# Two transformer blocks on one core: how the first input, the tables and the first matmuls are started

## The chip, the cores and the metric

The kernel runs on one core of a Trainium2 chip. The metric is the device time of one execution in microseconds. TensorE (PE) multiplies matrices, VectorE (DVE), ScalarE (ACT) and GpSimd (POOL) work element by element, and SyncE (SP) issues transfers. Transfers issued by SyncE and by ScalarE go into two queues (q1 and q10 in the profile), which the core's 16 DMA engines serve.

## The reference, cut to what matters

Two transformer blocks work one after the other on 1024 tokens of width 1024, in float32. Only the very beginning of the first block concerns this change:

```
n = rms_norm(x, attn_norm_w)      # x * rsqrt(mean(x * x) + eps) * w
proj = n @ w_in                   # keys, values, queries, retention heads, gates
aq, ak, av, rq, rk, rv, rg = split(proj)
aq, ak = rope(rms_norm(aq, q_norm_w)), rope(rms_norm(ak, k_norm_w))
```

After it come windowed attention, retention, an output projection, a feed-forward layer, and a second block with dilated attention, a gating unit, cross attention and a feed-forward layer.

## The kernel before, in words

**Layout.** The activations lie transposed: H is 128 partitions x 8 tiles (`kt`) x 1024 tokens. Tokens are worked on in two halves of 512 (`half(0)`, `half(1)`). `x_piece(t, q)` is a quarter of a tensor of that shape: q = 0 and 1 are tiles 0 to 3 and 4 to 7 of the first half of the tokens, q = 2 and 3 the same of the second. One piece is 1.05 MB, and each partition's rows in it are 2 KB long. ROPE (rotation tables) is 128 x 2 x 1024 floats, BD a 128 x 128 table, IDENT another, ONES 8 columns, VEC 117 columns. A unit of weights is 128 x 1024 floats, 0.52 MB.

**Precision.** Every float32 product is made of three fast matmuls. Each operand is split into a high part, rounded to the type of the fast matmul, and a low part, what is left. For a tile: WH x XH, WL x XH, WH x XL. GpSimd splits the weights (`split_unit`, L821 makes WH, L823 WL, a half unit at a time). ScalarE makes XH (`x_highs`, L1793 inside `high`), scaled by the norm's weight, and VectorE XL (`x_lows`, L2561 inside `low`), which needs XH. The division by the root of the mean square comes later, since it is one factor per token.

**First pass.** `first_units` (L1038, L1039, L1041) multiplies units 0 (keys) and 1 (values). For each half of the tokens it goes through the tiles with the two units side by side, the second unit three tiles behind the first: 48 matmuls per half. Ahead of the second half's first tile stand the column sums of squares of the first half (`norm_sums`, L1052), and ahead of its seventh tile the spreading of the reciprocal root over the partitions (`norm_spread`, L1071). TensorE's instructions run strictly in the order written.

**Orders on the other engines.** ScalarE: the issues of VEC, IDENT, ONES, the four pieces of H, BD and ROPE (L1821 to L1827), then high parts 0 and 1, squares 0 and 1 (L1839), high parts 2 and 3, square 2, the root, square 3. Its first real instruction loads an activation table (ACT_TABLE_LOAD). VectorE: four small edits of VEC (L2595 to L2598), low parts 0 and 1, the sums of squares 0 and 1 (L2608 to L2614), low parts 2 and 3, sum 2, a reciprocal, sum 3, then the evictions of the first pass (L2643). GpSimd: splits of units 0 and 1, and then one unit after another, each when TensorE has finished with that buffer. SyncE: units 0 and 1 (L734), then the next ones (L737), each after the split of the unit two before.

**Semaphores.** `vec_in` counts VEC, IDENT and ONES, and TensorE, ScalarE, VectorE and GpSimd all begin with a wait on it. `x_part[q]` tells that piece q of H is in. `x_in` is used much later for a reload of H (L2009, waited on at L3081). `dve_step` counts VectorE's own `link` steps. PS bank MB is the one that the column sums use later.

Of the kernel before, what the change touches and what calls it, by code (L numbers as in the profile page):

```python
# [23 lines left out]
ACT = mybir.ActivationFunctionType  # L24
# [3 lines left out]
P = 128  # L28
# [183 lines left out]
V_EPS = 114  # L212
# [4 lines left out]
C_ID, C_BD, C_ONE, C_MASK = 0, 128, 256, 384  # L217
# [86 lines left out]
def program(nc, xT, memT, ws, vec, cst, rope, bias, wsp, bsg, outT):  # L304
# [3 lines left out]
    def sem(name):  # L308
        return ctx.enter_context(nc.semaphore(name))

    with ctx:

        def sb(stack, name, shape, dt=F32):
            return stack.enter_context(nc.sbuf_tensor(name, shape, dt))
# [15 lines left out]
        SQ = sb(ctx, "SQ", [P, 2, HALF])  # L330
        XX = sb(ctx, "XX", [P, 2048])
        STAT = sb(ctx, "STAT", [P, 96])

        with ExitStack() as st:
# [7 lines left out]
            ROPE = sb(st, "ROPE", [P, 2, S])  # L342
            PT1 = sb(st, "PT1", [P, 3, 2 * P])
            BD = sb(st, "BD", [P, P])
# [14 lines left out]
        with ExitStack() as st:  # L359
            H = sb(st, "H", [P, KT, S])  # L360
# [47 lines left out]
        PS = ctx.enter_context(nc.psum_tensor("PS", [P, 8, HALF], F32))  # L408
        SB, OB, MB = 4, 6, 7
# [3 lines left out]
        def v(col, n=1):  # L413
            return VEC[:, col:col + n]

        def half(h):
            return slice(h * HALF, (h + 1) * HALF)
# [7 lines left out]
        vec_in, x_in, rope_in, mask_in, cst2_in, xr_in = map(sem, ("vec_in", "x_in", "rope_in", "mask_in", "cst2_in", "xr_in"))  # L425
        x_in2, bias_in0, bias_in1, sgu_in, mem_in = map(sem, ("x_in2", "bias_in0", "bias_in1", "sgu_in", "mem_in"))
        h_out, y_out = map(sem, ("h_out", "y_out"))
        x_part = [sem(f"x_part{q}") for q in range(4)]
# [12 lines left out]
        act_step, dve_step = map(sem, ("act_step", "dve_step"))  # L441
        vec_ready, blocks_in = map(sem, ("vec_ready", "blocks_in"))
# [90 lines left out]
        def x_piece(t, q):  # L533
            return t[:, 4 * (q % 2):4 * (q % 2) + 4, half(q // 2)]
# [51 lines left out]
        for g in range(3):  # L586
            q = 2 * (12 * g + 14)
# [144 lines left out]
        def _(sp):  # L732
            for j in range(2):
                sp.dma_start(WRAW[:, j], ws[WS_AT[j]]).then_inc(raw_in[j], 16)  # L734
            for u in range(2, U_RK):
                sp.wait_ge(unit_split, 2 * u - 2)
                sp.dma_start(WRAW[:, u % 2], ws[WS_AT[u]]).then_inc(raw_in[u % 2], 16)  # L737
# [249 lines left out]
        def _(pe):  # L987
# [101 lines left out]
                    unit_half(u, h, first_half_norm(k, 4, 6) if h else None)  # L1089


            pe.wait_ge(vec_in, 48)

            def scores1(s):
# [364 lines left out]
            def scores2(s):  # L1459
                g, b, j = place(s)  # L1460
                _, K, _ = QKV[g % 2]
                Q = QKV[g % 2][0]
                if g:
# [167 lines left out]
            for n in range(1, 4):  # L1631
                for h in range(2):
# [5 lines left out]
                    for b in range(2):  # L1638
                        for kt in range(KT):
                            last = pe.matmul(PS[:, MB, b:b + 1], XX[:, kt * MEM + b * P:kt * MEM + (b + 1) * P], ONES[:, 0:1],  # L1640
                                             start=(kt == 0), stop=(kt == KT - 1))
                    last.then_inc(mem_sum, 1)
                if n == 2:
                    pe.wait_ge(mem_inv, 1)
                    for b in range(2):
                        last = pe.matmul(PS[:, MB, blk(b)], STAT[:, 42 + b:43 + b].to_broadcast((P, P)), IDENT,
                                         start=True, stop=True)
# [125 lines left out]
        def _(act):  # L1773
# [18 lines left out]
            def high(dst, src, scale=1.0):  # L1792
                act.activation(dst, src, ACT.Copy, scale=scale).then_inc(x_high, 1)  # L1793
                nx.n += 1
# [26 lines left out]
            act.dma_start(VEC[:], vec).then_inc(vec_in, 16)  # L1821
            act.dma_start(IDENT, cst[:, C_ID:C_ID + P]).then_inc(vec_in, 16)
            act.dma_start(ONES, cst[:, C_ONE:C_ONE + NKEEP - P]).then_inc(vec_in, 16)
            for q in range(4):
                act.dma_start(x_piece(H, q), x_piece(xT, q)).then_inc(x_part[q], 16)
            act.dma_start(BD[:], cst[:, C_BD:C_BD + P]).then_inc(blocks_in, 16)
            act.dma_start(ROPE[:], rope).then_inc(rope_in, 16)  # L1827

            def x_highs(q):

                act.wait_ge(x_part[q], 16)
                for i in range(4):
                    kt, h = 4 * (q % 2) + i, half(q // 2)
                    high(XH[:, kt, h], H[:, kt, h], v(V_N1 + kt))

# [7 lines left out]
                act.activation(RST[h], PS[:, OB + h], ACT.Copy).then_inc(rst_made, 1)  # L1843

            act.wait_ge(vec_in, 48)
            x_highs(0)
            x_highs(1)
            x_square(0)
            x_square(1)
            x_highs(2)  # L1850
            x_highs(3)
            x_square(2)
# [472 lines left out]
            def copy_mb(k, n):  # L2325
                item = MB_USES.get(k, (None, None))[n]
                if item is None or item[0] == "mix":
                    return
                act.wait_ge(m_full, nm.n + 1)
                nm.n += 1  # L2330
                src = PS[:, MB].rearrange("p (a b) -> p a b", a=4)
                if item[0] == "v":
                    _, g, t, c = item
                    dst = QKV[g % 2][2][:, 4 * c:4 * c + 4, blk(t)]
                else:
                    _, t, c = item
                    dst = VS[:, 4 * c:4 * c + 4, blk(t)]
                act.activation(dst, src, ACT.Copy).then_inc(m_free, 1)
# [194 lines left out]
        def _(dve):  # L2533
# [5 lines left out]
            def link(ins):  # L2539

                ins.then_inc(dve_step, 1)
                nst.n += 1
                dve.wait_ge(dve_step, nst.at())
# [44 lines left out]
                        XH[:, m % 8, half(m // 8)])  # L2588


            dve.wait_ge(vec_in, 48)
            lf = VEC[:, V_LF:V_LF + 8]
            lfb = VEC[:, V_LFB:V_LFB + 16]
# [484 lines left out]
                    else:  # L3078
                        last_outputs()

            dve.wait_ge(x_in, 16)  # L3081
            dve.wait_ge(x_in2, 16)
            residual(U_WO1, 1)
            ffn(0, 1, V_F1, last_result1)
# [363 lines left out]
```

## Time and profile before

| | us |
|---|---|
| median of 3 runs | 2755.48 |
| lowest and highest | 2753.03, 2758.49 |
| the profiled execution, span | 2756.5 |
| TensorE busy in the span | 2702.0 |

The times above are whole executions, and the profile is one execution of its own: its span runs from its first instruction to its last. A row of the timeline gives the start in us from the span's start, the length, the engine, the line, the operation, the operands and how many are merged. A "q" behind an engine's name is its sequencer issuing transfers. In brackets stands how long the engine was idle before, and what ended it.

### The profile page before, as it was taken

The numbers are of one execution on the slowest core, as the hardware profiler recorded it, in microseconds if no ns is written. First come the engines' busy times: TensorE is split into PE (matmuls) and PEld (weight loads), VectorE is DVE, ScalarE is ACT, GpSimd is POOL, SyncE is SP. The second block draws the span as 40 slices with busy tenths as digits, with TensorE's granted clock in tenths as the row PEclk, the third lists the DMA queues.
The fourth block names the chain that finished last, engine by engine and source line by source line (L and its number), as shares of the span: only waits on it lengthen the run. The fifth ranks groups of instructions, "written<-read, shape, count | busy, mean of one in ns | idle before, by whom it ended". The sixth has DMA issues, their size and how long they took to land.

```text
span 2756.5 us, 37485 instructions
## 1 busy us (share of the span) xinstructions
PE 2702.0 (98%) x13788; PEld 2191.8 (80%) x13788; DVE 1719.8 (62%) x2578; ACT 1059.7 (38%) x2084; POOL 1518.5 (55%) x1148
## 2 busy tenths in 40 slices
PE   7999999999999999999999999999999999999998
PEld 6777788878888888777777788888788788888886
DVE  6776755687777777723355741143368777767777
ACT  5644422343444444423343511021254444444444
POOL 3232243477887878532222244455614788787884
PEclk9999999999999999999999999999999999999999
DMA  3001102111111211130101011131101212121112
GB/s 136 31 31 37 38 17 92 54 54 58 58 62 58 69 54 58 51 117 31 39 32 40 32 46 54 53 122 62 69 24 46 65 53 63 58 70 54 58 54 80
DMA packets 102774, 157.18 MB, mean 57 GB/s; under 512 B 6992, under 2 KB 60752, under 8 KB 101456
## 3 DMA queue, kind: packets, MB, share of 16 engines
q1 hardware_dynamic: 97472, 133.19, 14.5%
q10 hardware_dynamic: 5136, 21.76, 2.1%
q8 instruction: 106, 1.74, 0.3%
q14 instruction: 60, 0.49, 0.1%
HBM read 146.54 MB, written 8.39 MB: 56 GB/s over the span
## 4 chain that ended last, share of the span: by engine, by line
PE 91%; DVE 3%; POOL 2%; issue 1%; ACT 1%; DMA 1%; ACTq 0%; SPq 0%; DVEq 0%; POOLq 0%
PE PS L1346 13%; PE PS L1347 13%; PE PS L1348 13%; PE PS L1000 12%; PE PS L1002 11%; PE PS L1001 11%; PE PS L1120 1%; PE PS L1038 1%; PE PS L1041 1%; PE PS L1039 1%; PE PS L1109 1%; PE PS L1488 1%; PE PS L1380 1%; PE PS L1135 1%; PE PS L1374 1%
## 5 line engine op out<-in xcount | busy, mean ns | idle before, releaser
L821 POOL TENSOR_TENSOR WH<-WRAW,CST 128x512 fp32r<-128x512 f32 x204 | 226.5, 1110 | 838.9 <-PE PS L1002 725.7
L1000 PE MATMUL PS<-XH,WH 128*128 128x512 f32 x1248 | 513.4, 411 | 2.9 <-POOL WL L823 2.0
L1002 PE MATMUL PS<-XH,WL 128*128 128x512 f32 x1248 | 490.0, 393 | 0.0
L1001 PE MATMUL PS<-XL,WH 128*128 128x512 f32 x1248 | 488.8, 392 | 0.0
L3035 DVE TENSOR_TENSOR H<-H,PS 128x512 f32<-128x512 f32 x560 | 367.3, 683 | 41.9 <-PE PS L1348 41.7
L856 POOL TENSOR_TENSOR WL<-WRAW,WH 128x512 fp32r<-128x512 f32 x174 | 251.4, 1446 | 118.2 <-ACT WH L2058 88.8
L1000 PEld LDWEIGHTS PS<-XH,WH 128*128 128x128 f32 x1248 | 235.3, 189 | 82.8 <-issue 36.8
L823 POOL TENSOR_TENSOR WL<-WRAW,WH 128x512 fp32r<-128x512 f32 x204 | 271.3, 1330 | 16.0
L1002 PEld LDWEIGHTS PS<-XH,WL 128*128 128x128 f32 x1248 | 235.0, 188 | 51.4
L1001 PEld LDWEIGHTS PS<-XL,WH 128*128 128x128 f32 x1248 | 235.9, 189 | 41.9 <-issue 0.5
L856 POOL TENSOR_TENSOR WL<-XX,WH 128x512 fp32r<-128x512 f32 x148 | 202.0, 1367 | 92.9 <-ACT WH L2058 92.5
L1346 PE MATMUL PS<-XH,WH 128*128 128x512 f32 x640 | 249.5, 390 | 1.5 <-POOL WL L856 1.4
L1348 PE MATMUL PS<-XH,WL 128*128 128x512 f32 x640 | 249.2, 389 | 0.0
L1347 PE MATMUL PS<-XL,WH 128*128 128x512 f32 x640 | 249.2, 389 | 0.0
L1347 PE MATMUL PS<-PL,WH 128*128 128x512 f32 x624 | 243.2, 390 | 0.0
L1346 PE MATMUL PS<-PH,WH 128*128 128x512 f32 x576 | 224.7, 390 | 0.0
L1348 PE MATMUL PS<-PH,WL 128*128 128x512 f32 x576 | 224.3, 389 | 0.0
L1346 PE MATMUL PS<-TR,WH 128*128 128x512 f32 x480 | 187.9, 392 | 11.0 <-POOL WL L856 3.1
L1348 PE MATMUL PS<-TR,WL 128*128 128x512 f32 x480 | 187.4, 390 | 0.0
L1347 PE MATMUL PS<-TR,WH 128*128 128x512 f32 x480 | 187.4, 390 | 0.0
L2088 ACT ACTIVATE PH<-PV 128x512 fp32r<-128x512 f32 x140 | 88.2, 630 | 143.4 <-PE PS L1348 91.8
L1346 PEld LDWEIGHTS PS<-XH,WH 128*128 128x128 f32 x640 | 120.2, 188 | 27.5 <-issue 2.7
(371 smaller groups left out, 5416.0 us busy)
## 6 DMA issues: line engine op xcount, KB each, us to landing
WRAW<-ws SPq DMA_DIRECT2D x104, 512.0 KB, 3.5
WRAW<-ws SPq DMA_DIRECT2D x120, 256.0 KB, 2.6
XX<-ws SPq DMA_DIRECT2D x108, 256.0 KB, 2.7
RAWX<-ws SPq DMA_DIRECT2D x56, 256.0 KB, 2.6
H<-xT ACTq DMA_DIRECT2D x4, 1024.0 KB, 11.0
H<-xT ACTq DMA_DIRECT2D x2, 2048.0 KB, 11.1
h_spill<-H ACTq DMA_DIRECT2D x1, 4096.0 KB, 12.9
H<-h_spill ACTq DMA_DIRECT2D x4, 1024.0 KB, 8.5
```

The source lines that it names most:

```text
L821: pool.tensor_tensor(WH[:, j, c], WRAW[:, j, c], ONES[:, 0:1].to_broadcast((P, 512)), ALU.mult).then_inc(hi_split, 1)
L823: pool.tensor_tensor(WL[:, j, c], WRAW[:, j, c], WH[:, j, c].bitcast(F32), ALU.subtract).then_inc(unit_split, 1)
L856: pool.tensor_tensor(WLS[:, at], weight(s), WHS[:, at].bitcast(F32), ALU.subtract).then_inc(w_low, 1)
L1000: pe.matmul(out, WH[:, j, w], rh(kt), start=(n == 0), stop=False)
L1001: pe.matmul(out, WH[:, j, w], rl(kt), start=False, stop=False)
L1002: last = pe.matmul(out, WL[:, j, w], rh(kt), start=False, stop=(n == len(kts) - 1))
L1038: pe.matmul(PS[:, bank], WH[:, j, w], XH[:, kt, half(h)], start=(kt == 0), stop=False)
L1346: pe.matmul(PS[:, bank], WHS[:, at, w], xh, start=start and not on, stop=False, skip_group_check=on)
L1347: pe.matmul(PS[:, bank], WHS[:, at, w], xl, start=False, stop=False, skip_group_check=on)
L1348: return pe.matmul(PS[:, bank], WLS[:, at, w], xh, start=False, stop=stop, skip_group_check=on)
L2088: act.activation(PH[:, n % 2], value(name), ACT.Copy).then_inc(hid_high, 1)
L3035: dve.tensor_tensor(x, x, PS[:, 4 + t], ALU.add).then_inc(h_added, 1)
```

## The change

Five things are done together. The first piece of H comes in two transfers of two tiles each, with the semaphore `x_in` for the first (ScalarE waits for it, and for `x_part[0]` ahead of the third tile); the late wait on `x_in` goes up to 32. Pieces 2 and 3 of H, ROPE and BD are issued by SyncE right behind the first two units of weights, not by ScalarE. ScalarE runs one small copy as soon as the constants are in, before it waits for H. VectorE clears SQ[:, 0] first of all. And TensorE multiplies this cleared tile with itself five times, in plain float32 with 512 columns, into bank MB, before it waits for the constants.

```diff
--- before.py
+++ after.py
@@ -732,6 +732,10 @@
         def _(sp):
             for j in range(2):
                 sp.dma_start(WRAW[:, j], ws[WS_AT[j]]).then_inc(raw_in[j], 16)
+            for q in (2, 3):
+                sp.dma_start(x_piece(H, q), x_piece(xT, q)).then_inc(x_part[q], 16)
+            sp.dma_start(ROPE[:], rope).then_inc(rope_in, 16)
+            sp.dma_start(BD[:], cst[:, C_BD:C_BD + P]).then_inc(blocks_in, 16)
             for u in range(2, U_RK):
                 sp.wait_ge(unit_split, 2 * u - 2)
                 sp.dma_start(WRAW[:, u % 2], ws[WS_AT[u]]).then_inc(raw_in[u % 2], 16)
@@ -1089,6 +1093,9 @@
                     unit_half(u, h, first_half_norm(k, 4, 6) if h else None)
 
 
+            pe.wait_ge(dve_step, 1)
+            for n in range(5):
+                pe.matmul(PS[:, MB], SQ[:, 0, 0:P], SQ[:, 0], start=True, stop=True)
             pe.wait_ge(vec_in, 48)
 
             def scores1(s):
@@ -1821,15 +1828,16 @@
             act.dma_start(VEC[:], vec).then_inc(vec_in, 16)
             act.dma_start(IDENT, cst[:, C_ID:C_ID + P]).then_inc(vec_in, 16)
             act.dma_start(ONES, cst[:, C_ONE:C_ONE + NKEEP - P]).then_inc(vec_in, 16)
-            for q in range(4):
-                act.dma_start(x_piece(H, q), x_piece(xT, q)).then_inc(x_part[q], 16)
-            act.dma_start(BD[:], cst[:, C_BD:C_BD + P]).then_inc(blocks_in, 16)
-            act.dma_start(ROPE[:], rope).then_inc(rope_in, 16)
+            act.dma_start(H[:, 0:2, half(0)], xT[:, 0:2, half(0)]).then_inc(x_in, 16)
+            act.dma_start(H[:, 2:4, half(0)], xT[:, 2:4, half(0)]).then_inc(x_part[0], 16)
+            act.dma_start(x_piece(H, 1), x_piece(xT, 1)).then_inc(x_part[1], 16)
 
             def x_highs(q):
 
-                act.wait_ge(x_part[q], 16)
+                act.wait_ge(x_in if q == 0 else x_part[q], 16)
                 for i in range(4):
+                    if (q, i) == (0, 2):
+                        act.wait_ge(x_part[0], 16)
                     kt, h = 4 * (q % 2) + i, half(q // 2)
                     high(XH[:, kt, h], H[:, kt, h], v(V_N1 + kt))
 
@@ -1843,6 +1851,7 @@
                 act.activation(RST[h], PS[:, OB + h], ACT.Copy).then_inc(rst_made, 1)
 
             act.wait_ge(vec_in, 48)
+            act.activation(STAT[:, 57:58], v(V_EPS), ACT.Copy)
             x_highs(0)
             x_highs(1)
             x_square(0)
@@ -2588,6 +2597,7 @@
                         XH[:, m % 8, half(m // 8)])
 
 
+            link(dve.memset(SQ[:, 0], 0.0))
             dve.wait_ge(vec_in, 48)
             lf = VEC[:, V_LF:V_LF + 8]
             lfb = VEC[:, V_LFB:V_LFB + 16]
@@ -3078,7 +3088,7 @@
                     else:
                         last_outputs()
 
-            dve.wait_ge(x_in, 16)
+            dve.wait_ge(x_in, 32)
             dve.wait_ge(x_in2, 16)
             residual(U_WO1, 1)
             ffn(0, 1, V_F1, last_result1)
```

## Rows read from the trace of the kernel before

**Rows 1.** The page: span, and its section 4, the chain's shares by engine.
```profile
span 2756.5 us, 37485 instructions
...
PE 91%; DVE 3%; POOL 2%; issue 1%; ACT 1%; DMA 1%; ACTq 0%; SPq 0%; DVEq 0%; POOLq 0%
```

**Rows 2.** Chain of waits in order of time, first 27 us: start us, us, what.
```profile
2.16 8.06 DMA H<-xT
...
10.29 1.28 ACT L1793
...
12.34 5.74 DVE XL L2561 x4
...
18.13 0.49 PE PS L1041
```

**Rows 3.** Waits of PE, 18 to 47 us: us in total, times, longest us.
```profile
PE PS L1041 <- DVE XL L2561: 0.7, 1, 0.7
```

**Rows 4.** Windows: length, busy us (instructions) per engine, PEclk, DMA share, GB/s.
```profile
6.50:11.00 4.50, 0.00 (x0) 0.00 (x0) 1.27 (x4) 0.71 (x1) 3.86 (x4) 1.00 1.02 374
...
16.00:20.70 4.70, 3.97 (x16) 2.63 (x15) 4.70 (x7) 4.70 (x4) 1.52 (x1) 1.00 1.04 407
```

**Rows 5.** DMA queues (packets, MB, share) for 0 to 6, 3.5 to 5, 0 to 8.5 us.
```profile
q1 hardware_dynamic: 287, 1.05, 46.4%
q10 hardware_dynamic: 469, 0.25, 16.6%
...
q1 hardware_dynamic: 145, 0.53, 87.9%
q10 hardware_dynamic: 124, 0.05, 13.2%
...
q10 hardware_dynamic: 938, 1.15, 42.2%
```

**Rows 6.** Timeline of ACT, its queue and SyncE's queue, up to 60 us.
```profile
5.78 3.48 ACTq L1826 DMA_DIRECT2D BD<-cst  x1
...
11.59 5.01 ACT L1793 ACTIVATE XH<-H,VEC 128x512 fp32r<-128x512 f32 x8
11.72 36.37 SPq L737 DMA_DIRECT2D WRAW<-ws  x4
...
20.11 5.00 ACT L1793 ACTIVATE XH<-H,VEC 128x512 fp32r<-128x512 f32 x8
```

**Rows 7.** Timeline of DVE, 12 to 36 us.
```profile
12.34 8.38 DVE L2561 SCALAR_TENSOR_TENSOR XL<-H,VEC,XH 128x512 fp32r<-128x512 f32 x8 [4.14 <-ACT XH L1793]
...
24.48 0.69 DVE L2614 TENSOR_TENSOR ACC<-ACC,ROOM 128x512 f32<-128x512 f32 x1
25.09 5.38 DVE L2561 SCALAR_TENSOR_TENSOR XL<-H,VEC,XH 128x512 fp32r<-128x512 f32 x8
...
35.61 0.69 DVE L2643 TENSOR_TENSOR ACC<-PS,RG 128x512 f32<-128x512 f32 x1 [0.62 <-ACT RG L1843]
```

**Rows 8.** Timeline of POOL, its first and its last split of units 0 and 1.
```profile
6.98 1.04 POOL L821 TENSOR_TENSOR WH<-WRAW,CST 128x512 fp32r<-128x512 f32 x1 [6.53 <-DMA CST<-cst]
...
15.90 1.62 POOL L823 TENSOR_TENSOR WL<-WRAW,WH 128x512 fp32r<-128x512 f32 x1
```

**Rows 9.** Timeline of PE: column sums, spreading, end of the last early wait.
```profile
26.67 0.95 PE L1052 MATMUL PS<-CST,ACC 128*128 128x1 f32 x8
...
33.73 1.05 PE L1071 MATMUL PS<-CST,STAT 128*128 128x128 f32 x8
...
59.38 1.02 PE L1155 MATMUL PS<-BD,RQ 128*128 128x2 f32 x8 [1.70 <-ACT V L1910]
```

**Rows 10.** Windows as in rows 4: PE's first eight matmuls, and after 59.38.
```profile
12.45:16.40 3.95, 3.91 (x8) 2.13 (x8) 3.95 (x4) 3.95 (x7) 3.79 (x4) 1.00 1.05 396
61.00:64.00 3.00, 3.00 (x9) 2.35 (x8) 2.82 (x5) 1.95 (x4) 0.21 (x1) 0.50 0.47 162
```

**Rows 11.** Chain of waits as in rows 2: a plain float32 product, 512 columns.
```profile
44.84 0.86 PE PS L1152 x2
```

## Prediction, made before the change was built or run

> **What bounds the kernel now.** I read the page first, the chain of work that ended last second, and then one timeline per engine for the first 60 us. The page gives a 2756.5 us span and TensorE 91% of the chain [rows 1]. So the body is a serial queue of matmuls, and an edit to the first microseconds pays what it moves the start of that unbroken queue, and no more. The chain's opening shows where the queue starts [rows 2]: ScalarE's queue issues the first piece of H, its landing takes until 10.22, ScalarE loads its table (1.28 us), makes the first high part (VectorE can start at 12.34), VectorE makes four low parts (until 18.08), and from 18.13 TensorE has one matmul after another. Between 18 and 47 us TensorE waited for an engine once, 0.7 us, and that is the wait that ends at 18.13 [rows 3]. So the start that counts is 18.13, not the 12.45 of the first matmul. Twelve of the first pass's 48 matmuls are done by then; the other 36, 0.23 us apart, end at 26.6, when the column sums begin (26.67) [rows 9]. After about 47 us TensorE waits for VectorE and ScalarE (the last wait ends 59.38) [rows 9], and those waits hang on results that TensorE gave just before.
>
> **What the transfers do.** This decides the case. From 6.5 to 11 and from 16 to 20.7 us the DMA engines move 374 and 407 GB/s at a busy share of 1.02 and 1.04: they are full [rows 4]. By 6.0 us the sync queue (q1) has moved its 1.05 MB, both weight units, while ScalarE's queue (q10) has moved 0.25 MB, of which the small tables (253 columns of 128 rows) are 0.13 [rows 5]. After that q10 has the engines alone. Its 1.18 MB (tables and first piece) are through at about 8.6 (1.15 MB at 8.5) [rows 5], but the piece counts as landed at 10.22 [rows 2]: a tail of 1.65 us, since all 16 engines must finish. The second piece, another 1.05 MB at 0.39 MB per us (between the two of [rows 4]), is through at 11.3 and lands near 12.8. ScalarE asks for it at 14.1, after four high parts of 0.63 us (eight in 5.01) [rows 6], so nobody waits for it.
>
> **The change, part by part.**
>
> First piece in two transfers. Its first half is 0.52 MB. At 6.0 us 0.12 MB of it are in and 0.40 MB are left.
>
> Later tokens (2.1 MB), the rotation table (1.05 MB) and the block table on the sync queue. The sync queue held no transfer of its own from 6.0 to the issue at 11.72 [rows 5, 6]; now it has the third piece right behind the weights. How do two full queues share the engines? From 3.5 to 5.0 us they moved 145 and 124 packets [rows 5]: nearly one to one. The pieces have equal packets (2 KB rows) on both queues, so each queue gets half the bytes, some 0.19 MB per us. Hence: first half through at 6.0 + 0.40 / 0.187 = 8.15, landed with the same tail at 9.8; second half 2.7 us on, landed 12.5; **second piece, another 1.05 / 0.197 = 5.3 us on, landed at 17.7 instead of 12.8.** The bounds are 12.8 (the sync queue starts late or gets nothing) and 19.4 (the tail twice as long); I take the even share, which is what the nearest row shows. The issue of five more transfers on SyncE costs nothing: its next one waits until 11.72 anyway [rows 6], and the unit it fetches is split by POOL only when TensorE has ended the unit in that buffer, after both passes (past 36 us). ScalarE loses the block table's issue (3.48 us) and the rotation table's behind it, which ended ahead of 10.2 and were covered by the landing [rows 6].
>
> The Trainium skill ("DMA: Bandwidth & Descriptors", section "Issuing engines are not separate DMA queues") says that DMAs started by different engines run on the same 16 DMA engines and interleave, and that issuing on several saves only the issuing time. The rows agree as to the interleaving, and it speaks against the move: no bandwidth is added, and the urgent second piece now shares with tokens that ScalarE reads only at 20.1.
>
> Table load early. The constants are in at 6.5 (POOL's first wait) [rows 8], so the 1.28 us load runs from 6.9 to 8.2 while the transfer is in flight. It leaves the path entirely: the first high part ends at 9.8 + 0.73 = 10.5 instead of 12.32, the 0.73 being the way from the table's end at 11.57 to there [rows 2].
>
> Spare matmuls. A call with f32 operands and 512 columns is two instructions here, and two took 0.86 us of the chain [rows 11]. Five are 4.3 us at full rate. The first eight matmuls of the kernel before took 3.95 us [rows 10], 0.43 us apart and more: half the 0.23 us rate or less, though the granted clock reads 1.00 there; at half rate the five take 8.6 us. They start behind a memset at about 1.1 us and end between 5.4 and 9.7: ahead of 10.5. They cost nothing, but gain little too: TensorE was waiting for VectorE at 18.13, with the eight slow ones long behind it [rows 2, 9]. The memset is under 1 us on an idle VectorE.
>
> **The sum.** Low parts: the first four took 1.44 us each on the chain beside POOL's splits, and 0.66 after those end at 17.5 [rows 2, 7, 8]. From 10.5 four are ready at 16.3, not 18.08. But then the second piece is missing. High part four is done at 17.7 + 0.75 = 18.45, and TensorE (15 of 48 matmuls done) goes on with 33 x 0.23 = 7.6 us plus 0.3 us of waiting for the first low part: 26.3. ScalarE: four highs until 20.25, squares (1.8 us apart) until 22.15 and 23.95, where both were over by 20.2, since the third piece's high parts begin at 20.11 [rows 6]. VectorE's column sums of the first half of the tokens can end only 2.6 us after 23.95, at 26.6, where they ended at 25.17 [rows 7]; TensorE needs them at 26.67 in its order, so it loses nothing there. Then eight low parts (5.3 us) to 31.9, the third sum to 33.75, the reciprocal to 33.9: TensorE wants it at 33.73 [rows 9] and loses 0.2 us. The fourth sum ends at 36.6, the first eviction starts 1.0 us later than its 35.61, and that is slack for TensorE, whose first product from it comes at 44.84 [rows 7, 11]. So the 1.8 us gained ahead of 12 us are given back while waiting for the second piece: net **+0.2 us**. Span 2756.5 becomes 2756.7. The profiled span lies 1.0 us above the median of the runs, 2755.48, and inside their 2753.03 to 2758.49, so the forecast is 2755.48 + 0.2 = 2755.7.
>
> **Rivals.** (a) The second piece comes in time. If the sync queue's new transfers hardly get in, as bound 12.8, ScalarE never stops; four low parts are done at 16.3 minus the half microsecond that the warm matmuls save, 15.8, and TensorE's 36 matmuls end at 24.1 to 24.4: 2.3 us sooner, about 2753.2. For it: the count of 145 to 124 comes from small packets beside large ones, not from equals. Against it: the sync queue's weights, issued at the same time, were moving at full tilt from the start, and nothing in the trace holds its next transfers back. (b) Slower. TensorE stands thinly used for the 8 us before 18.4. After its wait up to 59.38 [rows 9] the granted clock was 0.50 from 61 to 64 us [rows 10]. If the clock falls likewise before 18.4, some eight matmuls at 0.43 instead of 0.23 put 1.7 us on top of 26.3, so the first pass ends at 28.0, and TensorE is 1.3 us behind; with the second piece 1 us later still it is 2.5 us: 2757 to 2758. It decides as soon as the fall costs more than the 0.35 us between 26.3 and the column sums' 26.65. The Trainium skill ("TensorE: Matmul & The Clock Gate", section "HAM oscillation — how this bites in real kernels") says waits on DMA between bursts let the clock fall again; no row here shows it for gaps as short as these. (c) The change does not do what it says: the spare matmuls end after 10.5, or the early load is followed by a second one ahead of the high parts. It costs at most the 1.28 us gained and hides behind the second piece: 2755.7 again, or 2754.5 beside (a).
>
> **How the numbers follow.** Forecast 0.50, (a) 0.27, (b) 0.15, (c) 0.08. All lie within 3 us of the start. The bound of 0.2%, about what a measurement can tell from no change, is 5.5 us, so what crosses it is the scatter of runs (2.5 us below and 3.0 above the median) on top of (a) or (b): faster 0.07, same 0.88, slower 0.05. The range takes (a) less 1.7 and (b) plus 1.7: 2751.5 to 2759.5.
>
> **What would show it.** Right: the H pieces' longest landing on ScalarE's queue near 15 us after issue; ScalarE idle about 3 us ahead of its third and again its fifth high part, with DMA named as what ended the wait; TensorE idle until 18.4; column sums at about 26.6; the chain naming the H transfer twice. Wrong: second piece landed before 14 us, TensorE unbroken from 16 us, column sums by 24.5 (rival a); the granted clock or the spacing at half rate beyond 18 us (rival b). The whole would be wrong by more than these sizes only if something outside the first 60 us moved, which no part of the change touches.

## The result, and the profile after

The changed kernel is slower, by 0.2%. Its 16 executions have a median of 2762.14 us (2755.91 to 2766.81) against 2755.85 us (2752.97 to 2760.86) for 16 of the kernel before; the ratio is 1.002, with a 95% interval of 1.0013 to 1.0026. Run again (e5 below) it came to 2761.02 against 2755.38, ratio 1.0019 (1.001 to 1.0028). The forecast was 2755.7 us in a range of 2751.5 to 2759.5. All medians below leave out four executions, one each in e1, e9, e10 and e11, that took 3007 to 12302 us.

The profiled execution is one of the quicker ones: 2757.94 us, with a span of 2756.1. That execution lasted 1.8 us longer than its span, and the profiled execution of the kernel before, with its span of 2756.5, was the one of 2758.49 us, 2.0 us longer. The two spans can't be compared by themselves; the first 60 us can.

Chain of waits of the changed kernel, first 60 us (start us, us, what), beside [rows 2]:

```profile
2.16 1.03 ACTq L1831
3.22 0.64 ACTq L1832
3.89 16.26 DMA H<-xT
20.17 0.73 ACT XH L1800
21.04 0.66 PE PS L1042
21.70 0.43 PE PS L1043
...
24.68 0.23 PE PS L1045
...
30.39 0.79 PE PS L1056 x8
```

The chain no longer runs through the first piece of H. It runs through the second: issued at 3.89, landed at 20.15. TensorE's unbroken queue starts at 21.04, not 18.13, and its first matmuls are 0.43 us apart. The column sums come 3.6 us later than in [rows 9].

Timeline of ScalarE in the changed kernel, beside [rows 6]:

```profile
4.41 1.28 ACT L1854 ACT_TABLE_LOAD   x1 [4.41 <-issue]
7.90 0.20 ACT L1854 ACTIVATE STAT<-VEC 128x1 f32<-128x1 f32 x1 [2.21 <-DMA CST<-cst]
10.60 1.34 ACT L1800 ACTIVATE XH<-H,VEC 128x512 fp32r<-128x512 f32 x2 [2.50 <-DMA H<-xT]
13.41 1.34 ACT L1800 ACTIVATE XH<-H,VEC 128x512 fp32r<-128x512 f32 x2 [1.47 <-DMA H<-xT]
20.17 2.56 ACT L1800 ACTIVATE XH<-H,VEC 128x512 fp32r<-128x512 f32 x4 [5.42 <-DMA H<-xT]
```

The table load is off the path: it ran from 4.41, before the constants were in. The first high part starts 1 us earlier than 11.59. But ScalarE, which made eight high parts in one go before, now stands idle three times for a landing, the last time for 5.42 us.

TensorE in the changed kernel (the spare matmuls, the restart behind the second piece, and the column sums):

```profile
1.46 7.54 PE L1098 MATMUL PS<-SQ 128*128 128x512 f32 x10 [1.46 <-DVE SQ L2600]
...
21.04 0.66 PE L1042 MATMUL PS<-XH,WH 128*128 128x512 f32 x1 [2.85 <-ACT XH L1800]
...
24.48 0.44 PE L1045 MATMUL PS<-XL,WH 128*128 128x512 f32 x1
...
30.22 0.95 PE L1056 MATMUL PS<-CST,ACC 128*128 128x1 f32 x8
```

Windows of the changed kernel (columns as in rows 4):

```profile
21.00:24.40 3.40, 3.37 (x8) 2.59 (x9) 2.66 (x4) 3.40 (x4) 0.00 (x0) 0.52 0.29 116
```

The granted clock is 0.52 of full speed for the 3.4 us behind the restart, that is at its lower level, 1.2 GHz, after TensorE had stood from 18.2 to 21.04 and been busy for 2.0 of the 3 us ahead of that.

The queues of the changed kernel (packets, MB, share of the 16 engines), beside [rows 5]: in order 0 to 6 us, 6.5 to 11 us, 16 to 18 us.

```profile
q1 hardware_dynamic: 356, 1.19, 52.4%
q10 hardware_dynamic: 317, 0.13, 8.6%
...
q1 hardware_dynamic: 488, 0.97, 57.3%
q10 hardware_dynamic: 452, 0.80, 48.0%
...
q1 hardware_dynamic: 81, 0.66, 80.2%
q10 hardware_dynamic: 80, 0.16, 21.7%
```

These rows bear on the working of the landing. By 6.0 us ScalarE's queue has moved 0.13 MB, not 0.25: its small tables themselves went slower, since the sync queue never ran dry. They were in at 7.9 us, where they had been in at 6.9. From 6.5 to 11 us the bytes are shared nearly evenly, as forecast. From 16 to 18 us the packets are still shared one to one, 81 to 80, but not the bytes: 0.66 MB against 0.16. The mean packet on q1 is then 8 KB. That is the rotation table, whose rows are 8 KB each, against the 2 KB rows of the second piece of H.

### The profile page after: what moved, and what is told of

Its sections match the earlier page's. It is cut to its first block, busy times and chain, and to the rows that moved or that the text cites. A ratio compares the mean times of both kernels' runs of the same rounds, so it can differ in the third digit from the quotient of the medians.

```text
span 2756.1 us, 37508 instructions
## 1 busy us (share of the span) xinstructions
PE 2706.1 (98%) x13798; PEld 2190.4 (79%) x13798; DVE 1719.6 (62%) x2579; ACT 1060.1 (38%) x2085; POOL 1520.8 (55%) x1148
## 4 chain that ended last, share of the span: by engine, by line
PE 91%; DVE 3%; POOL 2%; issue 1%; ACT 1%; DMA 1%; ACTq 0%; SPq 0%; DVEq 0%; POOLq 0%
PE PS L1353 13%; PE PS L1354 13%; PE PS L1355 13%; PE PS L1004 12%; PE PS L1006 11%; PE PS L1005 11%; PE PS L1127 1%; PE PS L1042 1%; PE PS L1045 1%; PE PS L1043 1%; PE PS L1116 1%; PE PS L1495 1%; PE PS L1387 1%; PE PS L1142 1%; PE PS L1381 1%
## 6 DMA issues: line engine op xcount, KB each, us to landing
h_spill<-H ACTq DMA_DIRECT2D x1, 4096.0 KB, 12.5
```

## The experiments

Each kernel ran beside the kernel before, in four groups (e1 to e4; e5 to e8; e9 and e10; e11 and e12), so that differences of about 1 us between groups mean little. "Sums" is the start of the first column sums in the one execution that was profiled (26.67 before); "piece 1" is when the second piece of H was in, read from ScalarE's next high part.

| kernel | piece 1, us | sums, us | median against before, us | ratio (95% interval) |
|---|---|---|---|---|
| changed, first time | 20.15 | 30.22 | +6.3 | 1.002 (1.0013 to 1.0026) |
| e5, changed again | 20.73 | 29.75 | +5.6 | 1.0019 (1.001 to 1.0028) |
| e1, all but the move | in time | 27.68 | +1.1 | 1.0007 (0.9998 to 1.0017) |
| e2, the move alone | 20.26 | 29.89 | +4.3 | 1.0016 (1.0007 to 1.0025) |
| e3, spare matmuls alone | in time | 26.74 | +1.0 | 1.0003 (0.9994 to 1.0012) |
| e4, SyncE held for piece 1 | 12.15 | 25.39 | -2.2 | 0.9993 (0.9984 to 1.0002) |
| e6, changed, no spares | 21.06 | 32.44 | +5.9 | 1.0015 (1.0006 to 1.0024) |
| e7, e4 without spares | 12.14 | 24.33 | -2.8 | 0.9989 (0.998 to 0.9998) |
| e9, four more spares | 20.85 | 30.45 | +4.8 | 1.002 (1.0011 to 1.003) |
| e11, two more spares | 20.77 | 29.79 | +5.0 | 1.0014 (1.0005 to 1.0024) |
| e8, only tables held | 17.32 | 26.41 | +1.7 | 1.0007 (0.9998 to 1.0016) |
| e10, table in 2 KB rows | 19.36 | 28.38 | +2.1 | 1.0007 (0.9998 to 1.0017) |

For e5 the sums had been expected between 30.2 and 32.2 us, with half rate behind the restart. They came at 29.75 and TensorE was at full rate there, so that failed; the median, expected 4 to 7 us above before, held.

### Taking the change apart

The first question was whether the move of transfers or the spare matmuls cost the time. e1 takes the move out:

```diff
-            for q in (2, 3):
-                sp.dma_start(x_piece(H, q), x_piece(xT, q)).then_inc(x_part[q], 16)
-            sp.dma_start(ROPE[:], rope).then_inc(rope_in, 16)
-            sp.dma_start(BD[:], cst[:, C_BD:C_BD + P]).then_inc(blocks_in, 16)
...
             act.dma_start(x_piece(H, 1), x_piece(xT, 1)).then_inc(x_part[1], 16)
+            for q in (2, 3):
+                act.dma_start(x_piece(H, q), x_piece(xT, q)).then_inc(x_part[q], 16)
+            act.dma_start(BD[:], cst[:, C_BD:C_BD + P]).then_inc(blocks_in, 16)
+            act.dma_start(ROPE[:], rope).then_inc(rope_in, 16)
```

> All of the change but the move: pieces 2 and 3 of H, BD and ROPE stay on ScalarE's queue behind piece 1; the split first piece, the early table load, the memset and the five spare matmuls stay in. Theory 1 (the second piece of H lands late because the sync queue's transfers take half of the DMA engines): the second piece lands near 12.8 us instead of 20.2, the first column sums come at 24.4 to 24.8 us (before 26.67, changed kernel 30.39), and the time is 2 us below the kernel before. Theory 2 (the spare matmuls or the clock behind them cost the time): column sums stay near 30 us and the time stays some 4 to 6 us above the kernel before.

e2 is the kernel before with the move alone:

```diff
+            for q in (2, 3):
+                sp.dma_start(x_piece(H, q), x_piece(xT, q)).then_inc(x_part[q], 16)
+            sp.dma_start(ROPE[:], rope).then_inc(rope_in, 16)
+            sp.dma_start(BD[:], cst[:, C_BD:C_BD + P]).then_inc(blocks_in, 16)
...
-            for q in range(4):
+            for q in range(2):
                 act.dma_start(x_piece(H, q), x_piece(xT, q)).then_inc(x_part[q], 16)
-            act.dma_start(BD[:], cst[:, C_BD:C_BD + P]).then_inc(blocks_in, 16)
-            act.dma_start(ROPE[:], rope).then_inc(rope_in, 16)
```

> The kernel before with the move alone: pieces 2 and 3, ROPE and BD on the sync queue behind the first two units of weights; no split, no early table load, no spare matmuls. Theory 1: the first piece lands near 13.5 us instead of 10.2 and the second near 20; column sums at 30 us or later, time 3.5 to 6 us above the kernel before. Theory 2: column sums within 1 us of 26.67, time unchanged.

e3 is the kernel before with the memset and the spare matmuls alone:

```diff
+            pe.wait_ge(dve_step, 1)
+            for n in range(5):
+                pe.matmul(PS[:, MB], SQ[:, 0, 0:P], SQ[:, 0], start=True, stop=True)
             pe.wait_ge(vec_in, 48)
...
+            link(dve.memset(SQ[:, 0], 0.0))
             dve.wait_ge(vec_in, 48)
```

> The kernel before with the memset and the five spare matmuls alone. Theory 1: nothing is moved by more than 1 us; column sums between 26.0 and 26.7 us, time within 1 us of the kernel before. Theory 2: the time rises by 2 us or more, and the trace shows TensorE at half rate in a place where it runs at full rate in the kernel before.

The move costs 4.3 us by itself, with an interval clear of no change, and shows the late piece without any other part. Chain of waits and then ScalarE's timeline in e2:

```profile
2.16 11.08 DMA H<-xT
```

```profile
14.60 2.56 ACT L1797 ACTIVATE XH<-H,VEC 128x512 fp32r<-128x512 f32 x4
20.28 2.56 ACT L1797 ACTIVATE XH<-H,VEC 128x512 fp32r<-128x512 f32 x4 [3.12 <-DMA H<-xT]
```

The first piece lands at 13.24 and the second at 20.26; 13.5 and 20 were expected. The sums, expected at 30 or later, came at 29.89. The spare matmuls alone moved the column sums by 0.1 us, and their time can't be told from no change. So theory 1 stands and theory 2 falls as an account of the loss. But e1 missed its numbers: it should have been 2 us quicker than the kernel before and is not, and its sums came at 27.68, not at 24.4 to 24.8. ScalarE's timeline in e1 tells why:

```profile
5.45 1.60 ACTq L1832 DMA_DIRECT2D BD<-cst  x1
7.09 2.55 ACTq L1833 DMA_DIRECT2D ROPE<-rope  x1
9.67 1.28 ACT L1854 ACT_TABLE_LOAD   x1 [9.67 <-issue]
...
11.07 5.00 ACT L1796 ACTIVATE XH<-H,VEC 128x512 fp32r<-128x512 f32 x8
```

The issues of BD and ROPE held ScalarE until 9.64. In the kernel before the landing of the first piece covered them. With half a piece that lands sooner (8.2 us) they are the next thing late: the table load came at 9.67 all the same, and the first high part starts only 0.5 us earlier than before. And TensorE fell to half rate after the spare matmuls. Windows of e1 and of e3:

```profile
13.70:20.40 6.70, 6.03 (x14) 3.71 (x13) 6.70 (x8) 6.70 (x8) 3.50 (x3) 0.50 1.04 402
```

```profile
12.00:18.00 6.00, 5.92 (x12) 2.99 (x12) 6.00 (x5) 6.00 (x9) 5.15 (x4) 0.50 1.05 396
```

The spare matmuls are done at 8.7 and 7.7 us; TensorE is then idle for 3.2 and 4.2 us, and the clock is at its lower level when the real work comes, or soon after, for 6.8 us. In e1 that outlasts VectorE's slow low parts, and the column sums come 1 us later than before; that the half rate is the reason is read from the trace and wasn't tested by itself.

### Keeping the move, and letting the second piece go first

e4 adds one wait to the changed kernel, e7 takes the memset and the spare matmuls out of e4 as well:

```diff
+            sp.wait_ge(x_part[1], 16)
             for q in (2, 3):
                 sp.dma_start(x_piece(H, q), x_piece(xT, q)).then_inc(x_part[q], 16)
```

> The changed kernel with one wait more: SyncE issues pieces 2 and 3, ROPE and BD only when piece 1 has landed. Theory 1: piece 1 lands near 12.8 us, piece 2 near 18, column sums at 24.4 to 24.8 us, time about 2 us below the kernel before, as in the run with the pieces on ScalarE's queue. Theory 2: as the changed kernel, 4 to 6 us above the kernel before.

> The changed kernel with SyncE held until piece 1 has landed, and without the memset and spare matmuls. Theory 1a: column sums at 25.4 us or earlier (with the spare matmuls 25.39), the time 2 to 3 us below the kernel before. Theory 1b: column sums at 26 us or later.

e6 is the changed kernel without the memset and the spare matmuls, with its transfers as they are; e7 has this edit too.

```diff
-            pe.wait_ge(dve_step, 1)
-            for n in range(5):
-                pe.matmul(PS[:, MB], SQ[:, 0, 0:P], SQ[:, 0], start=True, stop=True)
...
-            link(dve.memset(SQ[:, 0], 0.0))
```

> The changed kernel without the memset and the five spare matmuls. Theory 1a (the spare matmuls only start the clock early, and it falls again before it is needed): column sums within 0.7 us of the changed kernel's 30.39, the time the same as the changed kernel's or up to 2 us less, because TensorE's first 15 matmuls then run at half rate while it waits anyway, and it is at full rate at 21. Theory 1b (they do help): column sums and time 1.5 us or more later than with them.

ScalarE's timeline in e7:

```profile
8.24 2.65 ACT L1798 ACTIVATE XH<-H,VEC 128x512 fp32r<-128x512 f32 x4 [1.37 <-DMA H<-xT]
12.16 2.57 ACT L1798 ACTIVATE XH<-H,VEC 128x512 fp32r<-128x512 f32 x4 [1.27 <-DMA H<-xT]
```

With SyncE's later transfers held, the small tables are in at 6.7 us, the first half piece lands at 8.21 and the second piece at 12.14. The one wait turns +5.6 us into -2.2 us in e4. That is clearly quicker than the changed kernel, but its interval against the kernel before reaches 1.0002, and its sums came at 25.39, not at the 24.4 to 24.8 expected. e7, at -2.8 us with an interval below 1, is quicker than both kernels. What the split first piece and the early table load each bring of that wasn't tested. This is the version to keep. Its chain shows the next bound:

```profile
8.24 0.73 ACT XH L1798
...
8.99 10.84 DVE XL L2568 x8
19.83 1.14 DVE XX L2615
```

VectorE makes eight low parts in 10.84 us beside GpSimd's splits, 1.36 us each, where eight took 5.38 us later on [rows 7]. The column sums wait for VectorE's sums of squares behind them, not for TensorE's own matmuls.

The spare matmuls are worth nothing that the times show: e7 against e4 is -2.8 to -2.2 us, e6 against the changed kernel +5.9 to +5.6. The single traces differ in both directions by the clock. In e4 the fall to half rate came at 15.5 us, so its column sums are 1.1 us later than those of e7, where TensorE was at half rate only at its start, while VectorE was the bound anyway. In e6 TensorE was at the lower level through these 6.7 us behind the restart:

```profile
21.30:28.00 6.70, 6.05 (x14) 4.75 (x15) 5.23 (x7) 6.70 (x8) 0.00 (x0) 0.50 0.15 59
```

and its column sums came 2.2 us after those of the changed kernel, 0.9 us of which is a later landing. Expectation 1a said 0.7 us at most for the sums, and that failed; for the time it held.

### What made the second piece so late

e8 holds only ROPE and BD until piece 1 is in; pieces 2 and 3 go out at once.

```diff
+            sp.wait_ge(x_part[1], 16)
             sp.dma_start(ROPE[:], rope).then_inc(rope_in, 16)
             sp.dma_start(BD[:], cst[:, C_BD:C_BD + P]).then_inc(blocks_in, 16)
```

> The changed kernel with only ROPE and BD held on the sync queue until piece 1 has landed; pieces 2 and 3 go out at once. It parts the two reasons for the landing of piece 1 at 20.2 us instead of the 17.7 forecast. If the rotation table's larger packets (8 KB against 2 KB, one against one) take the last stretch, piece 1 lands at 18.5 to 19.3 and the column sums come about 1 us before 30.4. If only the late start of the first piece on the queues (7.5 us instead of 6.0) did it, piece 1 lands at 20 and nothing moves.

e10 leaves everything where it is and sends the rotation table in 2 KB rows:

```diff
-            sp.dma_start(ROPE[:], rope).then_inc(rope_in, 16)
+            for a in range(2):
+                for h in range(2):
+                    sp.dma_start(ROPE[:, a, half(h)], rope[:, a, half(h)]).then_inc(rope_in, 16)
...
-            dve.wait_ge(rope_in, 16)
+            dve.wait_ge(rope_in, 64)
```

> The changed kernel with ROPE issued as four transfers with rows of 2 KB in place of one with rows of 8 KB; nothing else. If the queues share the engines packet by packet, whatever the packets' size, piece 1 now keeps half of the bytes to its end and lands at 18.3 to 19.2 us instead of 20.2 to 20.7, and the time falls by 1 to 2 us. If the table's bytes count and not its packets, nothing moves.

Piece 1 in e8, and then in e10, by ScalarE's high parts (the first row starts with the second half of the first piece, the other with piece 1):

```profile
13.71 1.34 ACT L1801 ACTIVATE XH<-H,VEC 128x512 fp32r<-128x512 f32 x2 [1.46 <-DMA H<-xT]
17.34 2.57 ACT L1801 ACTIVATE XH<-H,VEC 128x512 fp32r<-128x512 f32 x4 [2.30 <-DMA H<-xT]
```

```profile
14.12 1.33 ACT L1802 ACTIVATE XH<-H,VEC 128x512 fp32r<-128x512 f32 x2 [1.45 <-DMA H<-xT]
19.38 2.56 ACT L1802 ACTIVATE XH<-H,VEC 128x512 fp32r<-128x512 f32 x4 [3.93 <-DMA H<-xT]
```

The queues from 11 to 17 us, in the changed kernel and then in e10:

```profile
q1 hardware_dynamic: 485, 1.42, 61.6%
q10 hardware_dynamic: 487, 0.96, 43.7%
...
q10 hardware_dynamic: 590, 1.18, 53.7%
q1 hardware_dynamic: 588, 1.14, 51.4%
```

In both kernels the packets go one to one, and only in e10 the bytes do too. So the engines were shared by packets whatever their size, and the table's large ones took part of the second piece's bandwidth.

What this is worth shows best from one landing on ScalarE's queue to the next, from the second half of the first piece to piece 1. It took 6.8 us in the changed kernel (13.41 to 20.17; 6.9 to 7.1 in e5, e6, e9, e11 and e12), 5.3 us in e10 and 3.6 us in e8. The large rows therefore cost 1.5 to 1.8 us. e8 gains 1.6 us more than e10 for another reason: its sync queue had only pieces 2 and 3 to move and moved nothing from 16 to 18 us.

Both expectations missed in part. In e8 piece 1 came at 17.3, sooner than the 18.5 to 19.3 expected, and the sums 4 us ahead of 30.4, not 1. In e10 19.36 is just past 19.2, and the time fell by 3.5 to 4.2 us where 1 to 2 were expected: +2.1 us instead of +5.6 to 6.3. In e8 it is +1.7, although its column sums are 0.3 us earlier than those of the kernel before. Neither e8 nor e10 can be told from the kernel before, since both intervals take in 1.

### The clock behind the wait

The last question was how much of the loss is the half rate after 21 us. e9 puts four more spare matmuls where TensorE waits for the second piece, e11 two.

```diff
+                            if (u, h, kt) == (0, 0, 4):
+                                for n in range(4):
+                                    pe.matmul(PS[:, MB], SQ[:, 0, 0:P], SQ[:, 0], start=True, stop=True)
                             pe.wait_ge(x_high, xs + 8 * h + kt + 1)
```

> The changed kernel with four more spare matmuls of the same kind between tile 3 and tile 4 of the first pass, where TensorE waits for the second piece (17.8 to 21 us in the changed kernel's profile). If the half rate behind that wait is the second half of the loss, there is no half-rate stretch after 21, column sums come at 29.5 to 30.2 in every execution, and the median falls by 1.5 to 2.5 us against the changed kernel's 5.6 to 6.3 above the kernel before. If the clock there is not part of it, the median stays where it is.

> The changed kernel with two spare matmuls more ahead of tile 4, where four ran past the landing of the second piece (until 23.1 us) and held TensorE up themselves. Two end before 21. If the half rate behind the wait is a part of the loss, the median comes 1 to 2.5 us below the changed kernel's, at 3 to 5 us above the kernel before; if it is not, the median stays at 5.5 to 6.3 above.

TensorE in e9, then in e11:

```profile
19.25 3.87 PE L1043 MATMUL PS<-SQ 128*128 128x512 f32 x8
...
30.45 0.95 PE L1059 MATMUL PS<-CST,ACC 128*128 128x1 f32 x8
```

```profile
19.18 2.46 PE L1043 MATMUL PS<-SQ 128*128 128x512 f32 x4
...
29.79 1.05 PE L1059 MATMUL PS<-CST,ACC 128*128 128x1 f32 x8
```

Four held TensorE until 22.55 and so stood in the way themselves. Two let it go on at 21.56, 0.05 us after high part four, and in both kernels it was at full rate from there on. The medians are +4.8 us (e9) and +5.0 us (e11) against before. For e11 that is the edge of the 3 to 5 expected; e9 fell by 0.8 to 1.5 us against the changed kernel, where 1.5 to 2.5 were expected, and its sums came at 30.45, not at 29.5 to 30.2. The half rate behind the wait is real in some executions, but taking it away brought 0.6 to 1.5 us, which these runs can't tell from nothing.

There is a reason why it can't bring more. In e5, where TensorE was at full rate anyway, the chain to the column sums doesn't run through its matmuls:

```profile
20.75 2.56 ACT XH L1800 x4
23.32 1.81 ACT XX L1847
...
29.00 0.70 DVE ACC L2624
29.75 1.05 PE PS L1056 x8
```

ScalarE's squares stand behind the four high parts of the second piece, and VectorE's sums of squares behind them. From the start of those high parts to the column sums it is 9.0 us in e5, e10 and e11, where TensorE was at full rate. It is 10.1 us in the changed kernel and e12, with 3.4 us at half rate, and 11.4 us in e6, with 6.7. So half rate behind the restart costs 1.1 us at the sums in the changed kernel and 2.4 us in e6.

e12 is one more execution of the changed kernel.

> One more look at the changed kernel, for where its executions differ. The second piece lands between 20.1 and 20.9 us; behind it TensorE runs at half rate for 0, 3.4 or 6.8 us, and the column sums come at 29.7, 30.4 or 32 us accordingly.

Its piece 1 landed at 20.8, it had half rate for 3.4 us behind the restart, and its column sums came at 30.87, 0.5 us past the 30.4 expected for that; piece 1 had landed 0.6 us later than in the first profile. It took 2756.95 us, again one of the quick ones. What these two quick ones have in common stands near 400 us. Windows of the kernel before, the changed kernel, e5 and e12, in this order:

```profile
394.00:408.00 14.00, 14.00 (x146) 13.27 (x147) 3.48 (x6) 2.36 (x4) 2.87 (x3) 0.63 0.00 1
```

```profile
394.00:408.00 14.00, 14.00 (x212) 13.06 (x210) 6.33 (x10) 3.94 (x6) 5.00 (x4) 1.00 0.01 2
```

```profile
394.00:408.00 14.00, 14.00 (x154) 13.14 (x152) 3.15 (x6) 2.95 (x6) 2.64 (x3) 0.76 0.01 1
```

```profile
394.00:408.00 14.00, 14.00 (x212) 13.11 (x210) 5.72 (x9) 3.94 (x6) 5.01 (x4) 1.00 0.01 2
```

At this place, the many small matmuls of retention, TensorE's clock is at its lower level for a part of the time in twelve of the fourteen traces of this case (0.63 to 0.88 in the window), and not at all in two, both of the changed kernel. Matched instruction by instruction on VectorE, the trace of the changed kernel is 3.6 us behind the trace of before at 45 to 60 us. It is 2.0 us behind from 70 to 390 us, since before has a half-rate stretch from 61 us on [rows 10] that the changed kernel lacks, and 2.8 us ahead from 409 us on. The stretch near 400 us alone is worth 4.8 us, almost as much as the whole effect, and it is why the span of the first profile hid the loss.

The scatter of the times goes with the clock in general. Of the 102 executions of the kernel before that ran beside the experiments, the 39 with a mean granted clock of 0.996 have a median of 2753.8 us, the 27 with 0.994 one of 2757.8 us. Which stretches differ in them is known only for the profiled ones.

## Why the prediction was wrong, point by point

**What bounds the kernel** held. The unbroken queue of matmuls starts when the last of the early results is in, and what moves its start moves the rest.

**The term that failed is the landing of the second piece.** The form was right: the sync queue's transfers take half of the engines, and ScalarE and TensorE stand until the piece is in. The size was not: 17.7 us forecast with 19.4 as the upper bound, 20.15 to 21.06 measured in six executions with these transfers (the changed kernel three times, e6, e9 and e11). Two things were missing in that step. First, I let ScalarE's queue start from the 0.25 MB that [rows 5] shows at 6.0 us. But that row belongs to a trace in which the sync queue runs out just then; with more behind the weights the small tables are in at 7.9 instead of 6.9, and the pieces start that much later. The second half of the first piece, forecast for 12.5, landed at 13.4 in the first profile and at up to 14.1 in the others, so this is worth 0.9 to 1.6 us. e4, which holds the later transfers, has its tables in at 6.7. Secondly, I took "one packet against one" and turned it into "half the bytes", which holds for the H pieces alone. I listed the rotation table among the moved transfers, wrote its size down, and never asked what its packets are. With equal rows (e10) piece 1 lands 5.3 us behind the second half of the first piece, where the forecast had 5.2, and with the 8 KB rows 6.8 to 7.1 us: 1.5 to 1.8 us more. The two together are the 2.5 us between 17.7 and 20.15, and the 3.4 us of the latest landing.

**The sum** fell with it. Column sums were forecast 0.1 us ahead of 26.67 and came at 29.75 to 30.87. In e5, where TensorE was at full rate behind the wait, high part four ends at 21.5 instead of 18.45, 3.0 us late, and the sums come 3.1 us late: all of it is the landing. They come by way of the squares, a path that the working had at 26.6 and so in time. In the first profile it is 2.5 us of landing, and the rest is the clock.

**Rival (b)** was a rival and became part of the case. The clock did fall while TensorE worked thinly and then waited (0.52 in the window behind 21 us), though in e5 it was at full rate there. I gave it 0.15 because its price alone, 1.3 to 2.5 us, didn't cross the bound; I did not ask what it would be on top of a later landing. Where the Trainium skill ("TensorE: Matmul & The Clock Gate", section "HAM oscillation — how this bites in real kernels") says that waits on DMA between bursts let the clock fall again, e3's trace agrees: TensorE stood for 4.2 us behind the spare matmuls while H was on its way, and was at half rate (0.50) from 12 us on. In e1 it stood for 3.2 us, for ScalarE's issues, and was at half rate 2 us after its restart. Rival (a), the second piece in time at -2.3 us, is what e4 and e7 are, at -2.2 and -2.8 us. Its price was right, in part by luck: the first half piece landed at 8.2, not 9.8, and what sets the sums in e7 is VectorE's low parts and sums of squares, not TensorE's 36 matmuls. The changed kernel isn't it.

**Single terms.** The constants were in at 6.9, not 6.5: the 6.53 of [rows 8] is the length of GpSimd's wait, not its end. Nothing hung on it, since the table load didn't wait for them. Table load off the path: right where BD and ROPE have left ScalarE's queue, and wrong without that (e1). I had priced their issues at nothing, since the landing covered them, which is so in [rows 6], but the cover goes when the first transfer shrinks. Spare matmuls: 7.54 us for ten instructions, inside 4.3 to 8.6, and no gain: right. SyncE's own issues: nothing, right. The memset: right (0.48 us). Two of the signs did not follow from the sum: the chain names the transfer of H once, not twice, and the sum itself had ScalarE idle for 1.4 us ahead of its third high part, not 3 (measured 1.47).

**The range.** The span of the profile was compared with the median of the runs as if the two were one measure. A span is 1.8 to 2.0 us short of its execution, so the profiled one stood 3 us above the median, and the two traces' spans say next to nothing at this size.

**What stays open.** The landing and the clock behind it explain 3.1 to 4.2 us at the column sums, and e6 shows 5.8. The medians are 5.6 and 6.3 us, which leaves 1.4 to 3.2 us. In the trace of e5 nothing is added after the column sums: it is 3.4 us behind the trace of before from 45 to 390 us. What is left goes with a lower mean granted clock over the whole execution (0.993 to 0.994 on average, 0.995 before; part of that is only that the spare matmuls make the first half-rate stretch count). Without spare matmuls the clocks can be compared. e2's executions are 4.0 us above those of before at a clock of 0.996 and 4.3 us at 0.994, so none of its 4.3 us is a lower clock. e6's are 3.5 and 4.0 us above (1.8 us at 0.995, where it has two), of 5.9 in all, so some 2 us of that would be that more of them ran at a lower clock. Whether a start 3 us later makes half-rate stretches more frequent, or this is chance, isn't shown.

## What to carry to other kernels

A transfer that is moved to a second queue isn't moved out of the way: here it ran beside the urgent one, and the queue with the longer rows got the more bytes. Before you spread loads over two queues, list in order of need what must land first, and let the rest wait for it with one semaphore; that one wait took the kernel from 5.6 us above the one before to 2.2 us below it (e4), and without the spare matmuls to 2.8 us below (e7). And an issue that was hidden behind a landing must be priced again when that landing becomes shorter.

## What the runs showed of the hardware

The two full queues shared the DMA engines packet by packet, whatever the packets' size: 81 to 80 packets were 0.66 to 0.16 MB (changed kernel, 16 to 18 us), 588 to 590 were 1.14 to 1.18 MB (e10, 11 to 17 us). An issue on ScalarE's queue behind all four pieces of H held the engine for 3.48 us (BD, before) or 2.55 us (ROPE, e1); on SyncE's queue, behind two units of weights and two pieces, the same two took 0.45 and 0.59 us. TensorE's clock, raised early by spare matmuls, was down to 0.50 again by 12 us in e3, 4.3 us after their end, with TensorE idle for 4.2 us of that. And the granted clock reads 1.00 ahead of the first change that a trace records, even where the matmuls' distance of 0.43 us shows half rate [rows 10].
